# Moving four gate panels from the attention loop into the head norms, the rotation and the turns of a two-block transformer kernel

## The chip, the cores and the metric

The kernel runs on one core of one Trainium2 chip. The metric is the device time of one execution in microseconds; lower is better.

## The reference, cut to what matters

All of it is float32, on 512 rows of width 1024. Two transformer blocks follow each other; the change touches one stretch of the first:

```python
u = rmsnorm(h, mix_norm)
(fq, fk, fv, ff, dq, dk, dv, iq, ik, iw, mq, g) = split(u @ w_in)   # g: 3 x 1024 gate columns
fq, fk = rmsnorm per head                                           # fox attention, 8 heads of 64
dq, dk = rope(rmsnorm per head);  iq, ik = rope(...)                # dsa attention, its index
mq, km = rmsnorm per head                                           # memory attention, 4 heads of 128
score = sum_h iw_h * relu(iq_h @ ik.T)                              # index scores, top 128 per query
o_a, o_b, o_c = fox, dsa (on the chosen keys), memory attention
h = h + sum_n(sigmoid(g_n) * (o_n @ w_branch_n)) @ w_out
```

The change concerns when `g = u @ w_in[:, gates]` is computed. It computes nothing else and leaves nothing out.

## The kernel before, in words

Everything is kept transposed: a tile has 128 features on the partitions and the 512 rows along the free dimension. A weight **panel** is 1024 x 128 (8 blocks of 128 x 128). Its product takes three float32r matmuls per block (`u_hi` with `w_hi`, `u_lo` with `w_hi`, `u_hi` with `w_lo`), 24 of 128x512 in one PSUM bank. A panel passes through a ring of four slots: SP loads `w_raw` (L432), ACT copies it into `w_hi` (`upper_part`, L459), DVE subtracts to make `w_lo` (`lower_parts`, L443), PE multiplies. ACT and DVE prepare panel n + 3 while panel n is multiplied; ACT may write a slot only after the panel that used it is done.

The 3 x 1024 gate columns are 24 panels of this kind. They are not multiplied in a stage of their own: `gate_panels_pe` (L361) is a generator that gives one block (three matmuls, L370 to L372) each time `feed` takes one from it, so that PE has something to do inside stages that wait for other engines. `gate_keep_dve` (L381, the instruction is L389) takes a finished panel out of its bank, `gate_upper` and `gate_lower` prepare the weights of panel m + 3. Gates 0 to 2 stay in SBUF, the others go to DRAM by `store_gate` and come back later. The order of every engine is written out by hand; semaphore counts tie the engines.

The stages around the change, in order of time:

- **mem_q**, the last of the ordinary projections, whose `uppers_act` and `keep_dve` leave gate panels 0 to 2 split.
- **Squares** (`squares_pe`, L750; batch 5, four blocks): ACT squares a head block (L748), PE sums over the features with 4 fp32 matmuls of 2 columns per block (L758) into bank 4. Then ACT takes roots (L764) and DVE one reciprocal (L783).
- **Head norms** (`block_norms_pe`, L766): for 21 blocks PE spreads the inverse roots over a bank (L777, banks 5 and 6 in turn), DVE multiplies (L787).
- **Rotation** (`rotate_pe`, L812): for 10 blocks PE makes the turned copy (L818, banks 4 and 5), DVE does three operations (L824 to L826). PE may start block e when DVE has finished block e - 2.
- **Turns** (`token_pe`, L830; "tokens"): ten groups of transposes (L839 to L845, banks 4 and 5), ACT copies each out (`token_act`, L853 to L863).
- **Index** (`index_pe`, L883): 32 score matmuls (L892), after each one block of a gate panel, after every fourth two: 40 blocks, 5 panels.
- **Attention** (`attend_pe`, L993): 20 steps, one per head: 8 fox, 4 memory, 8 dsa. A step is scores 3 and 2 (L1005), the turns of the step before (L1027), 4 gate blocks, scores 1 and 0, the product of the step before (L1041), 4 gate blocks, one turn. DVE takes maxima, ACT exponentials, POOL multiplies by the inverse sums. 19 gate panels are fed in steps 0 to 18; step 19 has none left.

Panels fed in the index stage and the loop use banks 2 and 3 (`gate_bank`, L323); the attention loop needs banks 0 to 2 for its turns.

Of the kernel before, what the change touches and what calls it, by code (L numbers as in the profile page):

```python
# [34 lines left out]
BANKS = 4  # L35
# [91 lines left out]
def build(nc, T, stop_at=None):  # L127
# [195 lines left out]
    def gate_bank(m):  # L323

        return ps[2 if m in (1, 3) else 3][:, :]
# [35 lines left out]
    def gate_panels_pe(pe):  # L361
        s = segs["gates"]
        for m in range(GATES):
            n = s.base + m
            pe.wait_ge(w_split, n + 1 + RING)
            pe.wait_ge(bank_read, s.group + BANKS + (m - 1 if 1 <= m < 5 else m))
# [14 lines left out]
    def gate_keep_dve(dve, m):  # L381
# [7 lines left out]
        dve.tensor_tensor(out, gate_bank(m), rms[:, :], ALU.mult).then_inc(bank_read, 1)  # L389

# [359 lines left out]
    def squares_pe(pe, blocks, batch, sq, mm):  # L750

        for i, e in enumerate(batch[1], batch[0]):
            x, rows, _, m = blocks[e]
# [12 lines left out]
    def block_norms_pe(pe, blocks, inv, bc, done):  # L766

        pe.wait_ge(inv, 1)
# [43 lines left out]
    def rotate_pe(pe):  # L812
        for e, (x, rows) in enumerate(rotated):
# [4 lines left out]
            pe.matmul(ps[4 + e % 2][0:rows, :], cst[0:rows, C_ROT:C_ROT + rows], x, start=True, stop=True).then_inc(rope_mm, 1)  # L818

    def rotate_dve(dve, st):  # L820
        dve.wait_ge(trig, 3)
        for e, (x, rows) in enumerate(rotated):
# [4 lines left out]
            dve.wait_ge(rope_done, e + 1)  # L827


    def token_pe(pe):  # L830
        pe.wait_ge(rope_done, NR)
        for e in range(10):
            if e >= 2:
                pe.wait_ge(token_done, e - 1)
# [64 lines left out]
    def index_act(act):  # L899
        n = 0  # L900
        for q in range(QB):
            w = (q + 1) * P
            for hh in range(8):
# [4 lines left out]
                if n in INDEX_UPPER:  # L908
                    gate_upper(act, INDEX_UPPER.index(n))
                n += 1  # L910

    def index_dve(dve, st):
        n = 0
        for q in range(QB):
            w = (q + 1) * P
            acc = probs[:, 1, q, :]
            for hh in range(8):
# [8 lines left out]
                if n in INDEX_KEEP:  # L926
                    gate_keep_dve(dve, INDEX_KEEP.index(n))
                if n in INDEX_UPPER:
                    gate_lower(dve, INDEX_UPPER.index(n))
# [63 lines left out]
    def attend_pe(pe, panels):  # L993
# [50 lines left out]
        for n in range(NJ):  # L1044
            scores(n, (3, 2))
            if n:
                turn(n - 1, (1, 0))
            feed(panels, 4)
# [3 lines left out]
            feed(panels, 4)  # L1052
# [4 lines left out]
    def attend_act(act):  # L1057
# [26 lines left out]
        for n in range(NJ):  # L1084
# [3 lines left out]
            if n + 5 < GATES:  # L1088
                gate_upper(act, n + 5)
# [19 lines left out]
    def attend_dve(dve, st):  # L1109
# [6 lines left out]
        for n, j in enumerate(jobs):  # L1116
            for q in DOWN:
                e = QB * n + DOWN.index(q)
                if q == 3:
                    gate_keep_dve(dve, n + 4)  # L1120
# [9 lines left out]
                if q == 2 and n + 5 < GATES:  # L1130
                    gate_lower(dve, n + 5)
# [998 lines left out]
    with block as blk:  # L2130
# [28 lines left out]
        def _(pe):  # L2159
# [14 lines left out]
            squares_pe(pe, head_norms, BATCHES[5], head_sq, head_mm)  # L2174
            block_norms_pe(pe, head_norms, head_inv, head_bc, head_done)
            rotate_pe(pe)
            token_pe(pe)
            panels = gate_panels_pe(pe)
            index_pe(pe, panels)
# [34 lines left out]
        def _(act):  # L2214
# [33 lines left out]
            roots_act(act, head_norms, head_mm, head_rt, root, HEAD_ROOTS)  # L2248
            act.wait_ge(trig, 1)
# [148 lines left out]
```

## Time and profile before

| | us |
|---|---|
| median of 3 runs (2581.49 to 2586.92) | 2586.06 |
| the profiled execution | 2585.37 |
| its span | 2583.6 |
| PE busy in the span | 2462.9 (95%) |
| DVE busy | 1344.5 (52%) |
| ACT busy | 879.4 (34%) |
| mean granted TensorE clock | 0.963 |

The span is what the profiler recorded on the core; 1.8 us lie around it. PE is busy in 95% of it, but a busy PE is not PE at its peak: matmuls are pipelined, and narrow ones (2 columns) count as busy like wide ones. The granted clock is 1.0 at 2.4 GHz and 0.5 at 1.2 GHz.

### The profile page before, as it was taken

To read this page: it belongs to the slowest core of one execution; us is meant where nothing else is said; L and a number is where in the kernel's file an instruction comes from. 1 tells how busy PE (TensorE), PEld (TensorE's weight loads), DVE (VectorE), ACT (ScalarE), POOL (GpSimd) and SP (SyncE) were. 2 spreads that over 40 slices of the span, in tenths; PEclk is the share of its full clock that TensorE was granted. 3 is DMA by queue.
4 is the path that set the end of the run, shared out by engine and by line. 5 is a ranking of instruction groups with operands and counts; after the bars stand their busy time and mean duration, and the time that the engine had idled before them with its cause. 6 is when DMAs were issued, how large, how long until landed. Compare 5 with 4: busy or idle time off the path is not lost.

```text
span 2583.6 us, 32030 instructions
## 1 busy us (share of the span) xinstructions
PE 2462.9 (95%) x12976; PEld 1948.6 (75%) x12976; DVE 1344.5 (52%) x2035; ACT 879.4 (34%) x1453; POOL 120.3 (5%) x156
## 2 busy tenths in 40 slices
PE   7999999997999999999999997888898899999997
PEld 6888888885566668888888886777776687788886
DVE  5444334436557447544433772433374763777723
ACT  4222223321344445322222433334246243433321
POOL 0000000000022210000000000222200000000000
PEclk9999999897999999999999996898898999999998
DMA  5333334330212125333333331000031132233331
GB/s 165 98 98 94 98 97 115 95 82 1 61 58 66 46 98 163 88 94 96 95 104 94 90 83 33 2 2 2 10 91 33 52 96 82 79 95 96 100 97 48
DMA packets 372466, 200.05 MB, mean 77 GB/s; under 512 B 12000, under 2 KB 364512, under 8 KB 372320
## 3 DMA queue, kind: packets, MB, share of 16 engines
q1 hardware_dynamic: 372320, 198.01, 26.5%
q8 instruction: 103, 1.69, 0.3%
q14 instruction: 43, 0.35, 0.0%
HBM read 190.38 MB, written 7.60 MB: 77 GB/s over the span
## 4 chain that ended last, share of the span: by engine, by line
PE 90%; DVE 6%; ACT 3%; issue 1%; DMA 0%; POOL 0%; DVEq 0%; SPq 0%; ACTq 0%
PE ps L510 21%; PE ps L511 21%; PE ps L512 21%; PE ps L370 2%; PE ps L1005 2%; PE ps L758 2%; PE ps L372 2%; PE ps L371 2%; PE ps L1041 2%; PE ps L777 1%; PE ps L2006 1%; PE ps L2008 1%; PE ps L2007 1%; PE ps L892 1%; PE ps L1500 1%; PE ps L1495 1%
## 5 line engine op out<-in xcount | busy, mean ns | idle before, releaser
L510 PE MATMUL ps<-u_hi,w_hi 128*128 128x512 f32 x1608 | 632.1, 393 | 3.0 <-DVE w_lo L443 2.1
L511 PE MATMUL ps<-u_lo,w_hi 128*128 128x512 f32 x1608 | 629.5, 391 | 0.0
L512 PE MATMUL ps<-u_hi,w_lo 128*128 128x512 f32 x1608 | 629.4, 391 | 0.0
L443 DVE TENSOR_TENSOR w_lo<-w_raw,w_hi 128x1024 fp32r<-128x1024 f32 (+2 forms) x366 | 423.0, 1156 | 306.7 <-ACT w_hi L459 305.6
L459 ACT ACTIVATE w_hi<-w_raw 128x1024 fp32r<-128x1024 f32 (+2 forms) x366 | 366.1, 1002 | 461.3 <-PE ps L512 432.6
L510 PEld LDWEIGHTS ps<-u_hi,w_hi 128*128 128x128 f32 x1608 | 300.1, 187 | 72.4 <-DVE w_lo L443 3.0
L511 PEld LDWEIGHTS ps<-u_lo,w_hi 128*128 128x128 f32 x1608 | 300.3, 187 | 67.8 <-issue 2.1
L512 PEld LDWEIGHTS ps<-u_hi,w_lo 128*128 128x128 f32 x1608 | 300.2, 187 | 67.8 <-issue 1.4
L512 PE MATMUL ps<-mid_hi,w_lo 128*128 128x512 f32 x528 | 208.6, 395 | 0.0
L510 PE MATMUL ps<-mid_hi,w_hi 128*128 128x512 f32 x528 | 208.6, 395 | 0.0
L511 PE MATMUL ps<-mid_lo,w_hi 128*128 128x512 f32 x528 | 208.5, 395 | 0.0
L510 PEld LDWEIGHTS ps<-mid_hi,w_hi 128*128 128x128 f32 x528 | 99.1, 188 | 24.1
L511 PEld LDWEIGHTS ps<-mid_lo,w_hi 128*128 128x128 f32 x528 | 99.1, 188 | 24.1
L512 PEld LDWEIGHTS ps<-mid_hi,w_lo 128*128 128x128 f32 x528 | 99.1, 188 | 24.1
L634 ACT ACTIVATE pair_a<-pair_a 128x512 f32<-128x512 f32 x44 | 27.9, 635 | 214.6 <-DVE pair_a L643 214.6
L1105 POOL TENSOR_TENSOR probs<-probs,stat 128x256 f32<-128x256 f32 (+1 forms) x80 | 56.0, 703 | 885.2 <-DVE stat L1114 885.2
L648 DVE TENSOR_TENSOR part<-ps,pair_b 128x512 f32<-128x512 f32 x44 | 30.4, 692 | 126.5 <-PE ps L512 126.4
L370 PE MATMUL ps<-u_hi,w_hi 128*128 128x512 f32 x192 | 84.5, 440 | 0.0
L1286 DVE SCALAR_TENSOR_TENSOR conv_t<-conv_in,vec,conv_t 128x512 f32<-128x512 f32 x108 | 81.0, 750 | 4.6 <-ACT conv_t L1268 2.0
L2092 ACT ACTIVATE conv_t<-conv_in,vec 128x512 f32<-128x512 f32 x44 | 36.0, 817 | 139.0 <-DVE conv_in L2107 139.0
L643 DVE TENSOR_TENSOR pair_a<-ps,rms 128x512 f32<-128x512 f32 x44 | 30.4, 691 | 95.5 <-PE ps L512 95.4
L372 PE MATMUL ps<-u_hi,w_lo 128*128 128x512 f32 x192 | 76.3, 397 | 0.0
(411 smaller groups left out, 3424.3 us busy)
## 6 DMA issues: line engine op xcount, KB each, us to landing
w_raw<-w_in_dram SPq DMA_DIRECT2D x101, 512.0 KB, 3.8
w_raw<-ffn_w_gate_dram SPq DMA_DIRECT2D x44, 512.0 KB, 3.9
w_raw<-ffn_w_up_dram SPq DMA_DIRECT2D x44, 512.0 KB, 3.8
w_raw<-w_up_dram SPq DMA_DIRECT2D x44, 512.0 KB, 3.7
w_raw<-ffn_w_down_dram SPq DMA_DIRECT2D x32, 512.0 KB, 3.7
w_raw<-w_out_dram SPq DMA_DIRECT2D x24, 512.0 KB, 3.6
w_raw<-w_down_dram SPq DMA_DIRECT2D x16, 512.0 KB, 3.6
w_raw<-ffn_w_down_dram SPq DMA_DIRECT2D x16, 384.0 KB, 3.3
```

Of the source, the lines that this page charges most:

```text
L370: pe.matmul(out, wh, u_hi[:, k, :], start=k == 0, stop=False)
L371: pe.matmul(out, wh, u_lo[:, k, :], start=False, stop=False)
L372: mm = pe.matmul(out, wl, u_hi[:, k, :], start=False, stop=k == DK - 1)
L443: dve.tensor_tensor(lo, raw, hi.bitcast(F32), ALU.subtract).then_inc(w_split, 1)
L459: act.activation(w_hi[:, n % RING, 0:blocks, 0:cols], w_raw[:, n % RING, 0:blocks, 0:cols], ACT.Copy).then_inc(hi_done, 1)
L510: pe.matmul(out, wh, h_k, start=k0 + k == 0, stop=False)
L511: pe.matmul(out, wh, l_k, start=False, stop=False)
L512: mm = pe.matmul(out, wl, h_k, start=False, stop=end)
L758: last = pe.matmul(ps[4][:, o:o + 2], square_room[i % 4][0:rows, u * P:(u + 1) * P], m[0:rows, :], start=True, stop=True)
L1005: mm = pe.matmul(bank[:, 0:w], j.q[:, q * P:(q + 1) * P], j.k[:, 0:w], start=True, stop=plain)
L1105: pool.tensor_tensor(x, x, r, ALU.mult).then_inc(sc_norm, 1)
L1286: dve.scalar_tensor_tensor(out=t, in0=x, scalar=v(wcol + n * taps + k), in1=t, op0=ALU.mult, op1=ALU.add).then_inc(conv_done if k == taps ...
```

## The change

Four of the nineteen panels fed in attention are fed earlier. Panels 0 to 3 are multiplied in the squares (one block ahead of each of the 4 squares), ahead of the head norms (6 blocks), in the rotation (2 blocks behind each of the 10 matmuls) and in the turns (2 blocks): 32 blocks. The index stage then multiplies panels 4 to 8, the attention loop panels 9 to 23 in the steps of `FED` (0 to 12, 14 and 16). Steps 13, 15, 17 and 18 now get none, as 19 before. Panels 0 to 8 go round the four banks 0 to 3, which the dense projections used, and wait only for the panel four groups back; from panel 9 on it is bank 3 alone. ACT gets `gate_upper(0)` behind the roots and `gate_upper(1)` to `(3)` behind the sine and cosine; DVE gets `gate_lower(0)` ahead of the reciprocal, and the other new `gate_keep_dve` and `gate_lower` as the diff shows.

```diff
     def gate_bank(m):
-        return ps[2 if m in (1, 3) else 3][:, :]
+        return ps[(segs["gates"].group + m) % BANKS if m <= 8 else 3][:, :]
...
             pe.wait_ge(w_split, n + 1 + RING)
-            pe.wait_ge(bank_read, s.group + BANKS + (m - 1 if 1 <= m < 5 else m))
+            pe.wait_ge(bank_read, s.group + m + (1 if m <= 8 else BANKS))
...
+    FED = tuple(range(12)) + (12, 14, 16)
+    def fed_panel(n):
+        return 9 + FED.index(n)
...
-    def squares_pe(pe, blocks, batch, sq, mm):
+    def squares_pe(pe, blocks, batch, sq, mm, panels=None):
         for i, e in enumerate(batch[1], batch[0]):
+            if panels:
+                feed(panels, 1)
...
-    def block_norms_pe(pe, blocks, inv, bc, done):
+    def block_norms_pe(pe, blocks, inv, bc, done, panels=iter(())):
+        feed(panels, 6)
         pe.wait_ge(inv, 1)
...
             pe.matmul(ps[4 + e % 2][0:rows, :], cst[0:rows, C_ROT:C_ROT + rows], x, start=True, stop=True).then_inc(rope_mm, 1)
+            feed(panels, 2)
...
             dve.wait_ge(rope_done, e + 1)
+            if e == 5:
+                gate_keep_dve(dve, 1)
-    def token_pe(pe):
+    def token_pe(pe, panels):
         pe.wait_ge(rope_done, NR)
         for e in range(10):
+            if e in (3, 6):
+                feed(panels, 1)
...
                 if n in INDEX_UPPER:
-                    gate_upper(act, INDEX_UPPER.index(n))
+                    gate_upper(act, 4 + INDEX_UPPER.index(n))
...
                 if n in INDEX_KEEP:
-                    gate_keep_dve(dve, INDEX_KEEP.index(n))
+                    gate_keep_dve(dve, 4 + INDEX_KEEP.index(n))
                 if n in INDEX_UPPER:
-                    gate_lower(dve, INDEX_UPPER.index(n))
+                    gate_lower(dve, 4 + INDEX_UPPER.index(n))
...
         for n in range(NJ):
+            blocks = 4 if n in FED else 0
             scores(n, (3, 2))
             if n:
                 turn(n - 1, (1, 0))
-            feed(panels, 4)
+            feed(panels, blocks)
             scores(n, (1, 0))
             if n:
                 product(n - 1)
-            feed(panels, 4)
+            feed(panels, blocks)
             turn(n, (2,))
...
-            if n + 5 < GATES:
-                gate_upper(act, n + 5)
+            if n in FED:
+                gate_upper(act, fed_panel(n))
...
-                if q == 3:
-                    gate_keep_dve(dve, n + 4)
+                if q == 3 and (n == 0 or n - 1 in FED):
+                    gate_keep_dve(dve, fed_panel(n - 1) if n else 8)
...
-                if q == 2 and n + 5 < GATES:
-                    gate_lower(dve, n + 5)
+                if q == 2 and n in FED:
+                    gate_lower(dve, fed_panel(n))
...
-            squares_pe(pe, head_norms, BATCHES[5], head_sq, head_mm)
-            block_norms_pe(pe, head_norms, head_inv, head_bc, head_done)
-            rotate_pe(pe)
-            token_pe(pe)
             panels = gate_panels_pe(pe)
+            squares_pe(pe, head_norms, BATCHES[5], head_sq, head_mm, panels)
+            block_norms_pe(pe, head_norms, head_inv, head_bc, head_done, panels)
+            rotate_pe(pe, panels)
+            token_pe(pe, panels)
...
             roots_act(act, head_norms, head_mm, head_rt, root, HEAD_ROOTS)
+            gate_upper(act, 0)
             act.wait_ge(trig, 1)
             act.activation(sinT, ang, ACT.Sin).then_inc(trig, 1)
             act.wait_ge(trig, 2)
             act.activation(cosT, turns_f, ACT.Sin, scale=-1.0).then_inc(trig, 1)
+            for m in (1, 2, 3):
+                gate_upper(act, m)
...
             dve.wait_ge(bank_read, segs["mem_q"].group + 4 + BANKS)
+            gate_lower(dve, 0)
             block_norms_dve(dve, head_norms, head_rt, len(HEAD_ROOTS), root, head_inv, head_bc, head_done)
+            gate_keep_dve(dve, 0)
             rotate_dve(dve, st)
+            gate_keep_dve(dve, 2)
+            for m in (1, 2, 3):
+                gate_lower(dve, m)
             dve.wait_ge(token_done, 12)
+            gate_keep_dve(dve, 3)
```

How the instructions stand, first on PE, from the last rows of the head norms through the start of the rotation. Before, the rotation (L818, `ps<-heads,cst`) is one row of matmuls behind another:

```order
L777 MATMUL ps<-cst,pair_b 64x128 x100
L777 MATMUL ps<-cst,pair_b 128x128 x24
L818 MATMUL ps<-heads,cst 128x512 x4
L818 MATMUL ps<-heads,cst 64x512
L818 MATMUL ps<-heads,cst 128x512 x4
```

In the changed kernel (its L786 and L827 are the L777 and L818 of before):

```order
L786 MATMUL ps<-cst,pair_b 64x128 x100
L786 MATMUL ps<-cst,pair_b 128x128 x24
L827 MATMUL ps<-heads,cst 128x512
L370 MATMUL ps<-u_hi,w_hi 128x512
L371 MATMUL ps<-u_lo,w_hi 128x512
L372 MATMUL ps<-u_hi,w_lo 128x512
L370 MATMUL ps<-u_hi,w_hi 128x512
L371 MATMUL ps<-u_lo,w_hi 128x512
L372 MATMUL ps<-u_hi,w_lo 128x512
L827 MATMUL ps<-heads,cst 128x512
```

Six gate matmuls stand between one rotation matmul and the next.

On DVE, from the last block kept of mem_q (L695) to the head norms, before:

```order
L443 TENSOR_TENSOR w_lo<-w_raw,w_hi 128x1024
L695 TENSOR_TENSOR heads<-ps,rms 128x512
L783 RECIPROCAL pair_b<-pair_b 128x168
L787 SCALAR_TENSOR_TENSOR heads<-heads,vec,ps 128x512 x12
```

and in the changed kernel:

```order
L701 TENSOR_TENSOR heads<-ps,rms 128x512
L449 TENSOR_TENSOR w_lo<-w_raw,w_hi 128x1024
L792 RECIPROCAL pair_b<-pair_b 128x168
L796 SCALAR_TENSOR_TENSOR heads<-heads,vec,ps 128x512 x12
```

A weight split now stands between the last block kept and the reciprocal for which the head norms on PE wait.

On PE in an attention step without panels, in the changed kernel (scores, turns of the step before, scores, first part of the product):

```order
L1019 MATMUL ps<-heads 128x384
L1027 MATMUL ps<-sel,cbf 128x384
L1041 MATMUL ps<-cst,probs 128x128 x7
L1019 MATMUL ps<-heads 128x256
L1027 MATMUL ps<-sel,cbf 128x256
L1019 MATMUL ps<-heads 128x128
L1025 MATMUL ps<-cbf 128x128
L1055 MATMUL ps<-keysT,dvt 64x512
```

This piece stood before in step 19 alone; it now stands in steps 13, 15, 17 and 18 too.

## Rows read from the trace of the kernel before

**Rows 1.** The page: busy time of PE, and its granted clock in 40 slices.

```profile
PE 2462.9 (95%) x12976; PEld 1948.6 (75%) x12976; DVE 1344.5 (52%) x2035; ACT 879.4 (34%) x1453; POOL 120.3 (5%) x156
...
PEclk9999999897999999999999996898898999999998
```

**Rows 2.** Stages: length, busy of PE, PEld, DVE, ACT, POOL, clock, DMA, GB/s.

```profile
574.30:581.30 7.00, 5.53 (x33) 5.43 (x32) 0.69 (x1) 3.47 (x5) 0.00 (x0) 0.72 0.03 8
581.30:583.80 2.50, 0.00 (x0) 0.00 (x0) 1.20 (x1) 2.46 (x8) 0.00 (x0) 0.50 0.00 0
583.80:605.60 21.80, 20.92 (x248) 18.71 (x248) 14.51 (x21) 1.23 (x2) 0.00 (x0) 0.91 0.01 2
605.60:628.70 23.10, 15.26 (x21) 3.56 (x21) 20.69 (x30) 0.00 (x0) 0.00 (x0) 0.78 0.00 1
628.70:636.70 8.00, 6.03 (x32) 4.46 (x32) 0.00 (x0) 5.44 (x12) 0.00 (x0) 0.71 0.00 0
636.70:645.70 9.00, 8.98 (x20) 5.64 (x21) 2.56 (x5) 2.05 (x5) 0.00 (x0) 0.50 0.00 1
645.70:698.10 52.40, 52.40 (x165) 26.14 (x163) 24.09 (x41) 17.48 (x33) 0.00 (x0) 1.00 0.20 55
```

**Rows 3.** Waits of PE, 574 to 960: total us, times, longest.

```profile
PE ps L818 <- DVE heads L826: 4.5, 7, 1.5
PE ps L839 <- DVE heads L826: 3.3, 1, 3.3
PE ps L777 <- DVE pair_b L783: 2.6, 1, 2.6
```

**Rows 4.** Timeline of PE, an earlier batch of four squares: start, us, instruction.

```profile
481.05 1.84 PE L758 MATMUL ps<-cst,pair_a 128*128 128x2 f32 x16
482.75 1.93 PE L758 MATMUL ps<-cst,pair_b 128*128 128x2 f32 x16
```

**Rows 5.** Timeline of ACT and DVE: one weight panel's two halves, and the reciprocal.

```profile
568.97 1.06 ACT L459 ACTIVATE w_hi<-w_raw 128x1024 fp32r<-128x1024 f32 x1 [4.38 <-PE ps L512]
...
570.06 1.23 DVE L443 TENSOR_TENSOR w_lo<-w_raw,w_hi 128x1024 fp32r<-128x1024 f32 x1 [0.46 <-ACT w_hi L459]
...
582.57 1.20 DVE L783 RECIPROCAL pair_b<-pair_b 128x168 f32<-128x168 f32 x1 [7.52 <-ACT pair_b L764]
```

**Rows 6.** Timeline of PE, score matmuls of the index stage.

```profile
636.72 0.79 PE L892 MATMUL ps<-heads 64*128 64x128 f32 x2 [1.46 <-ACT heads L863]
...
646.52 0.49 PE L892 MATMUL ps<-heads 64*128 64x128 f32 x2
...
647.83 0.48 PE L892 MATMUL ps<-heads 64*128 64x128 f32 x2
...
652.44 0.70 PE L892 MATMUL ps<-heads 64*128 64x256 f32 x2
...
687.04 1.12 PE L892 MATMUL ps<-heads 64*128 64x512 f32 x2
...
689.68 1.12 PE L892 MATMUL ps<-heads 64*128 64x512 f32 x2
```

**Rows 7.** Timeline of PE: start of steps 18 and 19.

```profile
922.08 1.12 PE L1005 MATMUL ps<-heads 64*128 64x512 f32 x2
...
935.05 1.12 PE L1005 MATMUL ps<-heads 64*128 64x512 f32 x2
```

**Rows 8.** Step 19: length, busy of PE, PEld, DVE, ACT, POOL, clock, DMA, GB/s.

```profile
935.05:942.60 7.55, 7.42 (x32) 3.74 (x32) 3.05 (x10) 3.96 (x12) 3.19 (x5) 1.00 0.59 188
```

**Rows 9.** PE in single microseconds: length, busy (instructions), granted clock, DMA, GB/s.

```profile
577.00:578.00 1.00, 1.00 (x9) 0.70 0.00 0
...
630.00:631.00 1.00, 1.00 (x6) 0.50 0.00 0
...
632.00:633.00 1.00, 0.78 (x5) 0.99 0.00 0
...
635.00:636.00 1.00, 0.26 (x4) 0.72 0.00 0
```

More of the change, by code:

```diff
@@ L810, in angles_dve, with rotate_pe @@
         dve.sem_inc(trig, 1)
-    def rotate_pe(pe):
+    def rotate_pe(pe, panels):
         for e, (x, rows) in enumerate(rotated):
```

## The prediction

> **What bounds the kernel now.** I read the busy times first: PE 95%, no other engine above 52% [rows 1]. So time is won only where PE waits, or where it runs at the lower clock; the line of granted clocks dips in two neighbourhoods, and the slices 9 to 11 (581 to 646 us and a little around) are the stretch that the change touches. Second, the windows by stage [rows 2]. From the end of mem_q (574) to the first score matmul (636.7) lie 62 us with a granted clock of 0.91 or less; the index stage starts with 9.0 us at 0.50 and is at 1.00 after that. Third, the waits of PE [rows 3]: within the stage it waits for DVE in the rotation (4.5 us), at the end of the rotation (3.3 us) and for the reciprocal (2.6 us). Over all five stages, length less busy time of PE in the windows, it comes to 14.7 us [rows 2]. Last, the attention loop: its dsa steps start at 922.08 and 935.05, 12.97 us apart; step 19, which has no panel, ends its last turn 7.55 us after its start, with PE busy 7.42 of that and the clock at 1.00 [rows 7, 8]. So a fed step is bound by PE's work alone, and the chain of DVE, ACT and POOL in an unfed one fits in PE's own 7.5 us.
>
> **What it removes.** Steps 13, 15, 17 and 18 lose 8 blocks each. The nearest row is step 19: 12.97 - 7.55 = 5.4 us a step, so 4 x 5.4 = 21.6 us. Three corrections. In step 19 the step before was fed, so the probabilities that it turns were long ready; with unfed steps in a row they are fresher. Step 19 already holds the whole chain of its own scores up to its last turn and waits 0.13 us in all, so I take as little again, 0.1 us a step, 0.4 us. In step 15, DVE also splits fox heads (twice two 128x512 operations, each 0.69 us or less by the rotation's 20.69 / 30 [rows 2]). They stand between one maximum and the next, with no gate matmuls left to hide them; 2.8 us is the upper bound and 0 the lower, and I take 1.0, since exponentials and copies of ACT cover part. Nothing saved at all would be the other bound (a step stays at 12.97); I go by step 19, which is the same code. Attention: 21.6 - 1.4 = **20.2 us less**.
>
> **What it adds: 32 blocks**, against the waits above. Stage by stage, at the full clock:
>
> - *Squares.* One square takes (482.75 - 481.05) / 2 = 0.85 us at the full clock [rows 4]. The first block runs in PE's wait for ACT's first square. A gate block among other matmuls costs 0.8 to 0.9 us: in the index stage a step with one block takes 1.31 us (646.52 to 647.83), of which 0.42 are the score [rows 6]. From 575.8: 4 x 0.85 + 3 x 0.8 = 5.8, end at 581.6 against 581.3: +0.3. Before, this stage was at 0.72 of the clock, which is why three more blocks cost so little.
> - *To the reciprocal.* Before, 2.5 us [rows 2]. Now ACT puts a `w_hi` copy (1.06 us) behind the roots, and DVE waits for it and subtracts (1.23 us) ahead of the reciprocal [rows 5]. The head norms wait for that reciprocal, so all of it is on the path: +2.4 with a semaphore. The six blocks (4.2 us) fit into the 4.9. Sum so far +2.7.
> - *Head norms.* PE sets their pace at the full clock (20.92 busy of 21.8 us). Before, the first two or so of 21 ran at 0.5: full clock from the start gives back 1.7. The keep of panel 0 lies beside the first rotation matmul. Sum +1.0.
> - *Rotation.* Before, DVE set the pace: 30 operations, 20.69 us busy in 23.1, so 2.18 us a block [rows 2]. Now PE does one 512-column fp32 matmul and two gate blocks per block. The nearest rows are the last steps of the index stage, 512 columns and two blocks: 687.04 to 689.68, 2.64 us [rows 6]. PE becomes the bound: 9 x 2.64, the last rotation (1.12) and DVE's three operations behind it (2.17), 27.05 us against 23.1. DVE has 0.46 us of slack a block, which takes in the keep (0.69) at block 5. +4.0, sum +5.0.
> - *Turns.* ACT sets the pace with its copies (5.44 of 8.0 us [rows 2]). Two gate blocks (1.7 us) lie beside them; DVE's two keeps and three splits, 2 x 0.69 + 3 x 1.23 = 5.1 us, were idle time of DVE before, and only the last keep comes after the turns, ahead of the first score that DVE waits for anyway. If the blocks were not hidden, +1.7; if the full clock makes the first transposes faster, -1.2. I take 0. Index starts at +5.0.
> - *Index.* The same 40 blocks. Before, the first four steps took 9.8 us (636.72 to 646.52) at 0.50, the next four 5.9 (to 652.44) at 1.00 [rows 6]: 3.9 us are there to be won, if the stage now starts at 2.4 GHz.
>
> DMA: each panel's load waits only for an earlier split, so loads and stores come earlier by up to four panels and nobody waits for them; DMA is at 0.20 in the index stage. The gate rows read back after the loop are stored earlier too. Cost 0.
>
> **The clock decides between three sums.** With 2.4 GHz held in both doubtful places: +5.0 - 3.9 - 20.2 = -19.1 us. If the index stage starts at 1.2 GHz as before: -15.2. If the clock also falls in the squares, where four squares of 2 columns before took it to 0.70 in the microsecond from 577 [rows 9] although PE was "busy": each square and block that remains takes nearly twice as long, about +3.6, for -11.6. For the index: in the turns the clock rose from 0.50 to 0.99 within a run of nothing but transposes (630 to 633), and fell again within the microsecond from 635, though transposes with short waits (0.78 busy in the microsecond from 632) had gone before [rows 9]. Two more gate blocks there do not make it dense, and in the last 1.5 us before the index PE waits for ACT's two copies as before [rows 6]. I take the fall as more likely than not (0.65), the one in the squares as slightly less likely than not (0.45), since 4 of its 7 us are now gate blocks or come right behind them.
>
> The Trainium skill has a rule on this (TensorE: Matmul & The Clock Gate, Part 4: PE-mode transpose): transposes do not count as PE activity for the clock gate and the full clock does not engage in them. By that rule the turns would always lose the clock, and the sum would be -15.2 at best; by the row, where transposes alone raised it, -19.1 stays open. That page and this trace differ, and the trace goes first.
>
> **Forecast.** The profiled execution took 2585.37, 0.7 below the median of 2586.06, so I work from it: 2585.4 - 15.2 = **2570.2 us**.
>
> **The rivals.**
> 1. *Both clocks held:* 2585.4 - 19.1 = 2566.3. For it: every wait in which the clock fell before is now filled or shorter. Against: the turns stay sparse.
> 2. *Both lost:* 2585.4 - 11.6 = 2573.8. For it: squares brought the clock down in this trace each time they ran.
> 3. *Unfed steps are bound by the chain.* In 17, 18 and 19 in a row, the chain maximum, exponential, inverse, POOL, turn, copy is not renewed behind gate matmuls. If a step then takes 10 us instead of 7.55, 4 x 2.4 = 9.8 of the gain go: 2580. Against: in step 19 PE waits 0.13 us in all, ACT is busy 3.96 and POOL 3.19 of 7.55 us [rows 8].
> 4. *Slower: the clock falls in the unfed steps.* What holds it in attention may be the gate matmuls, wide and dense; without them a step has narrow fp32 and transposes. At 0.50 an index step took 9.8 / 5.9 = 1.66 times as long, so a step 7.55 x 1.66 = 12.5, 5.0 more; in all five unfed steps 25 us: 2585.4 - 15.2 + 25 = 2595. It is slower from the fourth such step on. Against: step 19 at 1.00 [rows 8], and the head norms, fp32 with 128 columns alone, came from 0.50 to a mean of 0.91 without any gate block [rows 2].
> 5. *It does not do what it says* is excluded: the order of PE shows 32 blocks in the new places, and four steps without.
>
> **How the numbers follow.** Forecast 0.45 (index alone loses the clock, or the squares alone, nearly the same sum), rival 1 0.17, rival 2 0.26, rival 3 0.08, rival 4 0.04. The range 2562 to 2578: from rival 1 with 4 us more, for turns that run faster and unfed steps without my corrections, to rival 2 with 4 us for a rotation or turns that hide less. It leaves out rivals 3 and 4. A measurement here tells about 0.2%, 5.2 us, from no change. All of the forecast, rivals 1 and 2, and half of rival 3 are faster by more: 0.92; the other half of rival 3: same, 0.04; rival 4: 0.04.
>
> **What would show it.** Right: steps 13, 15, 17, 18 of 7.6 to 8.6 us in the timeline of PE at clock 1.00; rotation matmuls 2.6 us apart, with DVE idle in between; the reciprocal some 2.7 us later; the first score matmul near 641.7, 5 us later than before; the attention loop ending some 15 us earlier. Wrong: unfed steps above 9 us; a half clock in them or in the rotation, where each block would then take over 4 us; a wait of PE on a split weight or a bank in the first gate blocks.

## The result, and the profile after

| | before | changed |
|---|---|---|
| median when the change was first timed | 2583.77 us (4 runs) | 2561.73 us (2556.48 to 2564.09, 4 runs) |
| median in a second series | 2586.71 us (2581.21 to 2588.48, 11 runs) | 2561.85 us (2556.71 to 2566.46, 6 runs) |
| ratio, 95% interval | | 0.9911 [0.9891, 0.9932]; second series 0.9911 [0.9896, 0.9926] |

The change saves 22 to 25 us (0.9%), where 15.2 were forecast; 2561.73 lies 0.3 us below the range. The page of the changed kernel, busy times and granted clock, against [rows 1]:

```profile
PE 2441.7 (96%) x12976; PEld 1937.4 (76%) x12976; DVE 1343.4 (53%) x2035; ACT 878.9 (34%) x1453; POOL 120.5 (5%) x156
...
PEclk9999999999999999999999996988998999999998
```

The dip at slice 10, where the stretch that the change touches begins, is gone in this execution. The digit of slice 8 is 9 instead of 8, but that slice lies ahead of the change and the clock still falls there: it was at 0.5 for some 3 us each from 473 and from 484. The same stages as in [rows 2], now for the changed kernel: squares, wait for the reciprocal, head norms, rotation, turns, index, attention up to step 19. Columns are those of [rows 2].

```profile
573.60:580.90 7.30, 6.53 (x46) 5.68 (x45) 0.69 (x1) 3.48 (x5) 0.00 (x0) 1.00 0.03 8
580.90:585.50 4.60, 4.20 (x18) 3.10 (x17) 2.34 (x2) 4.54 (x10) 0.00 (x0) 1.00 0.00 1
585.50:605.65 20.15, 19.26 (x248) 16.84 (x248) 14.51 (x22) 1.06 (x2) 0.00 (x0) 1.00 0.10 27
605.65:629.90 24.25, 23.37 (x80) 14.44 (x80) 21.97 (x33) 2.12 (x2) 0.00 (x0) 1.00 0.00 0
629.90:637.85 7.95, 5.47 (x38) 4.25 (x38) 4.08 (x4) 5.29 (x12) 0.00 (x0) 1.00 0.63 168
637.85:695.40 57.55, 57.53 (x184) 29.45 (x184) 27.26 (x47) 19.56 (x38) 0.00 (x0) 1.00 0.25 73
695.40:911.60 216.20, 212.31 (x909) 131.90 (x908) 127.11 (x340) 91.14 (x236) 52.80 (x75) 1.00 0.18 55
```

To compare kernels I measure one **stretch** everywhere: from the start of DVE's keep of the last mem_q block (574.35 before, 573.64 after) to the first score of step 19 (935.05, 911.57). It is 360.70 us before and 337.93 in this profile. All numbers of the next table are differences of start times in the profiles; "reciprocal" is from that keep to the first head norm on PE, and the six stages add up to the stretch.

| profile | reciprocal | head norms | rotation | turns | index | attention | stretch |
|---|---|---|---|---|---|---|---|
| before | 9.5 | 21.8 | 23.1 | 8.0 | 61.4 | 236.9 | 360.7 |
| changed (first) | 11.9 | 20.2 | 24.3 | 8.0 | 57.6 | 216.1 | 337.9 |
| changed, again (after_again) | 16.2 | 20.1 | 24.3 | 8.0 | 60.5 | 216.2 | 345.2 |
| changed, third (after_third) | 11.9 | 20.1 | 24.3 | 8.0 | 57.6 | 216.1 | 337.9 |
| changed, fourth (changed_timed) | 11.9 | 20.2 | 24.3 | 8.0 | 62.0 | 216.2 | 342.5 |

The order of the instructions is the same in the last four rows, and four of the six stages repeat to 0.1 us. Only two stages move, and both with the granted clock.

What PE waits for, 574 to 960, changed kernel (total us, times, longest), the largest rows, against [rows 3]:

```profile
PE ps L1041 <- POOL probs L1120: 2.3, 3, 0.8
PE ps L906 <- ACT heads L877: 1.5, 1, 1.5
PE ps L1055 <- ACT keysT L1092: 1.1, 2, 0.8
PE ps L853 <- DVE heads L836: 0.9, 1, 0.9
```

The 4.5, 3.3 and 2.6 us of before have become nothing, 0.9 and 0.4 (the last, the wait for the reciprocal, is a smaller row of the same view).

### The profile page after: what moved, and what is told of

It is laid out like the page before. It is cut to its first block, busy times and chain, and to the rows that moved or that the text cites. A ratio compares the mean times of both kernels' runs of the same rounds, so it can differ in the third digit from the quotient of the medians.

```text
span 2554.7 us, 32031 instructions
## 1 busy us (share of the span) xinstructions
PE 2441.7 (96%) x12976; PEld 1937.4 (76%) x12976; DVE 1343.4 (53%) x2035; ACT 878.9 (34%) x1453; POOL 120.5 (5%) x156
## 4 chain that ended last, share of the span: by engine, by line
PE 91%; DVE 5%; ACT 3%; issue 1%; POOL 0%; DMA 0%; DVEq 0%; SPq 0%; ACTq 0%; POOLq 0%
PE ps L516 21%; PE ps L517 21%; PE ps L518 21%; PE ps L1019 2%; PE ps L370 2%; PE ps L766 2%; PE ps L1055 2%; PE ps L372 2%; PE ps L371 1%; PE ps L786 1%; PE ps L2021 1%; PE ps L2023 1%; PE ps L2022 1%; PE ps L906 1%; PE ps L1515 1%; PE ps L1510 1%
```

## The experiments

### What moving alone does: burst

```diff
-            squares_pe(pe, head_norms, BATCHES[5], head_sq, head_mm, panels)
+            squares_pe(pe, head_norms, BATCHES[5], head_sq, head_mm)
...
-        feed(panels, 6)
+        feed(panels, 32)
...
-            feed(panels, 2)          # rotation
+            feed(panels, 0)
...
-            if e in (3, 6):          # turns
-                feed(panels, 1)
```

> All 32 blocks in one burst between the squares and the head norms, none in the squares, the rotation and the turns; attention as in the changed kernel. Measured from the last block that DVE keeps of mem_q: first score (before 62.4 us, changed 64.2), index stage (61.4, 57.5), attention to the scores of step 19 (236.9, 216.1). Theory (the gain is that PE's waits and low clock are filled): the burst pays for itself, 21.8 us less the 2.5 us wait for the reciprocal and about 1.7 of clock, so first score near 80, the clock falls in the rotation as before and the index stage is 61.4 again, attention 216.1; sum 357 to 358, within 3 us of before. Rival (the attention loop was burdened by more than PE's own time of the panels, so that moving them anywhere wins): sum below 350.

Measured: stretch 360.0 us; first score at +82.2, index 61.7, attention 216.1; 2581.96 us in all beside 2586.91 of before. The stages: squares, burst, norms to turns, index:

```profile
574.40:581.40 7.00, 5.63 (x33) 5.63 (x34) 0.65 (x1) 3.47 (x5) 0.00 (x0) 0.71 0.02 5
581.40:604.60 23.20, 23.20 (x98) 18.83 (x98) 2.34 (x2) 7.83 (x13) 0.00 (x0) 0.94 0.08 23
604.60:656.50 51.90, 40.39 (x301) 24.91 (x300) 40.59 (x58) 5.43 (x12) 0.00 (x0) 0.83 0.11 28
656.50:718.00 61.50, 61.48 (x184) 31.98 (x184) 27.15 (x47) 19.35 (x38) 0.00 (x0) 0.92 0.23 67
```

Attention gives back its 20.8 us and the burst takes all of it; the stretch is 0.7 us shorter than before (2 to 3 us longer than I had computed, since the first score came at +82.2 and not near 80). Moving alone wins nothing in the stretch. What wins is where the same 32 blocks stand in the changed kernel: in waits, and in stages that ran at 1.2 GHz without them. burst does not tell these two apart, as it lost the clock in the squares, in the rotation (at 635.7) and again just ahead of the index stage (at 655.9). The whole run was 5 us below its run of before although the stretch was not; that part is taken up below (Outside the stretch).

### Does it repeat: after_again, after_third

> The changed kernel once more, for how far its stages repeat. If its granted clock is settled by the order of the work, the clock is 1.00 from mem_q to the branches again and the stages repeat within 0.2 us (64.2, 57.5, 216.1). If it was luck of this one execution, the index stage is 61.4 or the squares fall to 0.5 in this one.

> The changed kernel a third time. The first execution held 2.4 GHz from mem_q to the branches (337.9 us from the last kept block to the scores of step 19), the second lost it in the squares and at 643 (345.2). If which of the two comes is settled anew in each execution, this one lies at 337.9, 340.9 (index lost), 342.2 (squares lost) or 345.2, with attention at 216.1 and the rotation at 24.3 in each. If it is the chip that decides, it is 345.2 like the second.

Measured: 345.2, then 337.9 (the table above). In the second profile the clock fell in the squares and once more in the index stage; its stages from the squares to the norms, and the first 9 us of the index:

```profile
576.40:582.40 6.00, 5.99 (x31) 5.57 (x32) 0.00 (x0) 2.81 (x4) 0.00 (x0) 0.68 0.02 3
582.40:591.10 8.70, 8.70 (x29) 7.02 (x29) 2.34 (x2) 5.60 (x11) 0.00 (x0) 0.63 0.13 29
...
643.50:652.50 9.00, 8.98 (x24) 5.45 (x25) 3.17 (x6) 2.06 (x5) 0.00 (x0) 0.62 0.16 52
```

These profiles came from different chips, so by themselves they do not exclude the chip as the cause. Two other things do: of the kernels profiled on the chip of after_again, fed15 and split_behind kept the clock in the squares, after_again and index128 lost it there, and up to that point fed15, index128 and after_again are the same program; and six executions on one chip (changed_timed, below) spread over 9.8 us. So the clock is settled anew in each execution. Losing it in the squares costs 16.16 - 11.86 = 4.3 us, losing it in the index stage 2.9 to 4.4.

### What holds the clock: no_square_blocks, two_in_squares, no_turn_blocks, no_turn_again, one_in_rotation

```diff
# no_square_blocks: squares_pe without panels, and
-        feed(panels, 6)
+        feed(panels, 10)
# two_in_squares
-                feed(panels, 1)
+                feed(panels, 2)
-        feed(panels, 6)
+        feed(panels, 2)
# no_turn_blocks
-            if e in (3, 6):
-                feed(panels, 1)
-        feed(panels, 6)
+        feed(panels, 8)
# one_in_rotation: behind each rotation matmul, and ahead of the norms
-            feed(panels, 2)
+            feed(panels, 1)
-        feed(panels, 6)
+        feed(panels, 16)
```

> The 4 blocks between the squares go behind them (10 ahead of the head norms). Theory (those blocks keep TensorE at 2.4 GHz through the squares): the granted clock falls to 0.5 within the squares as before, squares take 5.5 us instead of the time with blocks, several of the ten blocks run at 1.2 GHz, and the head norms start about 3 us later than in the changed kernel; first score near 67. Rival (the clock does not hang on them): the head norms start within 0.7 us of the changed kernel, first score near 64.2.

> Two gate blocks ahead of each of the four squares, two ahead of the head norms. Theory (the share of wide matmuls between the squares decides whether the clock falls there): the clock stays at 1.00 through the squares; the squares end 2.0 us later (three more blocks on their path), the head norms start at +13.9 instead of +11.9, first score 66.2. Rival (the share does not matter): the clock falls at about 577 and the head norms start after +17.

Measured: without blocks the clock was lost at once and the norms started at +16.9, 5.0 us later than in the changed kernel and not 3; with two, it was held through the squares, the norms started at +13.9 as computed, but then the clock fell in the 2 us in which PE had nothing to do, and the first score came at +67.6 instead of 66.2 (the first line is no_square_blocks' squares; the others are two_in_squares' squares and blocks, its idle time, its first norms):

```profile
574.50:582.00 7.50, 6.09 (x33) 6.09 (x34) 0.69 (x1) 3.66 (x6) 0.00 (x0) 0.68 0.02 6
```

```profile
574.50:586.00 11.50, 10.64 (x62) 8.75 (x60) 0.66 (x2) 5.67 (x13) 0.00 (x0) 1.00 0.02 4
586.00:588.40 2.40, 0.01 (x2) 0.01 (x2) 2.34 (x2) 2.36 (x3) 0.00 (x0) 0.90 0.01 2
588.40:592.00 3.60, 3.60 (x40) 3.60 (x42) 0.92 (x2) 1.05 (x2) 0.00 (x0) 0.59 0.53 144
```

Over all profiles of this study: without a block between the squares the clock was lost in them in 3 of 3 (before, burst, no_square_blocks); with one block each, in 4 of 13; with two, in 0 of 1. That alone is few. The same traces hold more: the four earlier batches of four squares (from 469, 480, 507 and 518 us), which no kernel of this study changes and which have no gate block between them, lost the clock too. It fell some 2 to 5 us after their first matmul in 67 of 68 cases (four batches in 17 profiles). The theory stands, with the addition that one block leaves it to chance; what is said of two blocks rests on one profile.

> The 2 blocks of the turns go ahead of the head norms (8 there). Theory T (the two blocks keep the clock up through the turns): the granted clock falls near the end of the turns and the index stage takes 61.4 us as before. Rival R (the dense rotation does it, the turns are then too short for a fall): the index stage stays at 57.5, first score 63.5 to 65.

> no_turn_blocks a second time. The first lost the clock at 636 and its index stage took 61.9; the changed kernel lost it at 643 in one of three. Theory T (without wide matmuls in the turns the clock falls): index stage 60 or more again. Rival (chance): 57.6.

Measured: index stage 61.9 in both. The first 9 us of it in the first of them:

```profile
636.90:646.00 9.10, 9.10 (x21) 5.67 (x22) 3.24 (x6) 2.06 (x5) 0.00 (x0) 0.50 0.30 90
```

That agrees with T, but it does not tell it apart from chance: with the two blocks in the turns the clock was lost at the start of the index stage in 7 of 9 profiles too (those in which rotation, turns and the way into the index stage stand as in the change; wide_keys, which has one ACT copy fewer there, lost it as well). What the two blocks are worth for the clock stays open. In time they are worth nothing either way: the turns took 6.9 us instead of 8.0, the norms started 0.9 us later, and the first score came at +64.1.

> One block instead of two behind each rotation matmul, the other ten ahead of the head norms (16 there). If PE's time of a 128-row rotation matmul with its blocks is what I now read (0.88 us and 0.68 a block, 2.24 for two), the rotation is bound by DVE again at 2.18 us a block, 0.7 us shorter in all, and the ten blocks ahead of the norms cost 6.8 less the 0.4 us wait: first score near 70. The clock: with PE busy some 1.7 of 2.2 us it holds and the index stage is 57.5; the rival is a fall as before (first score near 71, index 61.4).

Measured: first score +71.9. Norms at +18.2 and the rotation 23.6 us came as computed; PE, timeline, shows DVE in the lead again, 2.17 us apart with a wait before each:

```profile
618.38 1.13 PE L827 MATMUL ps<-heads,cst 128*128 128x512 f32 x2 [0.36 <-DVE heads L836]
620.55 1.07 PE L827 MATMUL ps<-heads,cst 64*64 64x512 f32 x2 [0.35 <-DVE heads L836]
```

The clock fell at 635.6 here, in the last microsecond of the rotation, so that most of the turns ran at 1.2 GHz (10.0 us instead of 8.0), and was back before the index (57.6): neither of my two cases.

### Why the rotation was cheaper than forecast: index128

```diff
-        for b in (B_DKV, B_IKW):
-            act.activation(heads[64:128, b, :], heads[0:64, b, :], ACT.Copy).then_inc(token_done, 1)
+        for x, b in ((heads[64:128, B_DKV, :], B_DKV), (pair_a[64:128, 0, :], B_IKW)):
+            act.activation(x, heads[0:64, b, :], ACT.Copy).then_inc(token_done, 1)
...
-                pe.matmul(..., heads[r, B_IQ + hh // 2, q * P:(q + 1) * P], heads[r, B_IKW, 0:w],
+                pe.matmul(..., heads[:, B_IQ + hh // 2, q * P:(q + 1) * P], idx_keys[hh % 2][:, 0:w],
...
+    idx_keys = (heads[:, B_IKW, :], pair_a[:, 0, :])
...
+            dve.memset(pair_a[0:64, 0, :], 0.0).then_inc(keys_zero, 1)
+            dve.wait_ge(token_mm, 10)
+            dve.memset(heads[64:128, B_IKW, :], 0.0).then_inc(keys_zero, 1)
```

> The index scores use all 128 rows: the stationary block holds two heads, the moving keys are zero in the other head's half (a second key tile, two memsets of DVE). Same products. Theory (a matmul on 64 rows between matmuls on 128 costs about 0.4 us more than one on 128 rows, which is why my price for the rotation was too high): a step of 128 columns takes 0.9 us instead of 1.31, one of 512 columns with two blocks 2.24 instead of 2.64, the index stage 57.5 - 32 x 0.4 = 45 us. Rival (the 0.4 us is the change of kind, fp32 to float32r, and the rotation was cheap for another reason): index stage stays at 57.5.

In the changed kernel's own rotation, eight matmuls are on 128 rows and two on 64 (PE, timeline; `128*128` and `64*64` are rows by columns of the stationary block):

```profile
608.00 1.02 PE L827 MATMUL ps<-heads,cst 128*128 128x512 f32 x2
608.45 0.80 PE L370 MATMUL ps<-u_hi,w_hi 128*128 128x512 f32 x1
...
610.24 1.02 PE L827 MATMUL ps<-heads,cst 128*128 128x512 f32 x2
...
614.82 1.07 PE L827 MATMUL ps<-heads,cst 64*64 64x512 f32 x2
615.82 0.50 PE L370 MATMUL ps<-u_hi,w_hi 128*128 128x512 f32 x1
...
617.31 1.02 PE L827 MATMUL ps<-heads,cst 128*128 128x512 f32 x2
```

A block on 128 rows takes 2.24 us (608.00 to 610.24) and the next gate matmul starts 0.45 us behind it; on 64 rows it takes 2.49 and the gate matmul starts 1.00 behind, and the 64-row matmul itself starts some 0.1 us late (the block before it took 2.33). The index stage has 64-row matmuls only. Two of its steps in the changed kernel, and two in index128:

```profile
645.10 0.49 PE L906 MATMUL ps<-heads 64*128 64x128 f32 x2
...
646.41 0.49 PE L906 MATMUL ps<-heads 64*128 64x128 f32 x2
```

```profile
646.50 0.38 PE L909 MATMUL ps<-heads 128*128 128x128 f32 x2
647.43 0.38 PE L909 MATMUL ps<-pair_a,heads 128*128 128x128 f32 x2
```

1.31 us against 0.93, with the same number of columns and the same kinds of matmul beside it (2.64 against 2.25 for 512 columns and two blocks). Whether the 64 rows were the lower or the upper half made no difference: the steps before take 1.31 in turn. The whole stage took 46.6 us instead of 57.6 to 62.0, 2551.84 us in all. The theory holds; 45 was for the full clock, and this stage began with 3 us at 0.5. wide_and_ahead (below) has the full clock throughout and 43.8 us, but with 38 of the 40 blocks in the stage; with two more at 0.7 us each that is an estimated 45.2.

### Two small terms: fed15, split_behind

```diff
# fed15
-    FED = tuple(range(12)) + (12, 14, 16)
+    FED = tuple(range(13)) + (15, 16)
# split_behind: in block_norms_dve, behind the reciprocal instead of ahead of it
         dve.reciprocal(inverse[:, 0:n], root[:, 0:n]).then_inc(inv, 1)
+        gate_lower(dve, 0)
```

> Steps 15 and 16 are fed, 13, 14, 17, 18 and 19 not. Theory (step 15 took 8.30 instead of 7.61 us because DVE's split of the fox heads stands bare there): all unfed steps take 7.61, fed 15 and 16 12.98, attention 0.7 us shorter (215.4). Rival (the 0.7 us came from the step before or after): no change, the 0.7 us shows in another step.

In the changed kernel, step 15 (875.04 to 883.34, 8.30 us) shows DVE's split ahead of the maxima, and PE's two waits:

```profile
877.64 0.77 DVE L1178 TENSOR_TENSOR o_lo<-heads,o_hi 128x512 fp32r<-128x512 f32 x1
878.33 0.54 DVE L1137 TENSOR_REDUCE stat<-ps 128x1 f32<-128x384 f32 x1
```

```profile
879.64 0.48 PE L1019 MATMUL ps<-heads 64*128 64x128 f32 x2 [0.44 <-ACT probs L1080]
...
880.59 2.34 PE L1055 MATMUL ps<-keysT,dvt 128*64 128x512 f32 x8 [0.31 <-ACT keysT L1092]
```

In fed15 (steps 13 to 17 and the start of 18):

```profile
857.99 1.12 PE L1019 MATMUL ps<-heads 64*128 64x512 f32 x2
865.61 1.12 PE L1019 MATMUL ps<-heads 64*128 64x512 f32 x2
873.22 1.12 PE L1019 MATMUL ps<-heads 64*128 64x512 f32 x2
886.23 1.12 PE L1019 MATMUL ps<-heads 64*128 64x512 f32 x2
899.23 1.12 PE L1019 MATMUL ps<-heads 64*128 64x512 f32 x2
906.84 1.12 PE L1019 MATMUL ps<-heads 64*128 64x512 f32 x2
```

Unfed 7.61, 7.61 and 7.61, fed 13.0: attention 215.5, 0.6 us less. Step 15 costs more only when it is unfed, and DVE's split is what stands bare in it; no run took the split away by itself.

> DVE's split of panel 3 goes behind the reciprocal. Theory (the six blocks hide all but 0.4 us of it): head norms start 0.4 us earlier, first score 63.8. Rival (as I predicted, 1.2 us of it on the path): first score 63.0. Below, no effect.

Measured: norms at +11.4 instead of +11.9, first score +63.8, as the first theory had it. The run (2561.62 us) lost the clock in the index stage, so its total says nothing of 0.4 us.

### Can the start of the index be filled: ahead_of_index

```diff
     def index_pe(pe, panels):
+        feed(panels, 2)
         pe.wait_ge(token_done, 12)
...
-                feed(panels, 2 if n % 4 == 3 else 1)
+                feed(panels, (2 if n % 4 == 3 else 1) if n < 31 else 0)
```

> Two of the 40 blocks of the index stage go ahead of its wait for ACT's two copies, after the last turns. Theory (PE idles 1.5 us there, and that idle time is what brings the clock down at the start of the index stage): first score at most 0.1 us later than 64.2, the index stage 1.5 us shorter (56.0) and at 1.00 throughout. Rival (the fall comes from the turns themselves): 1.5 us shorter at full clock, but the clock falls again between 636 and 645 and the stage takes 59 to 60.

Measured: the first score came at +68.6, because this execution lost the clock in the squares. The index stage stayed at 1.00 and took 56.8 us, but attention took 219.4, 3.2 more. I had taken the two blocks from behind the last score. There PE now waits bare for ACT, 0.69 us, and the clock falls in the first attention step (index, boundary, step 0):

```profile
644.00:700.00 56.00, 56.00 (x179) 28.38 (x178) 26.45 (x46) 18.15 (x36) 0.00 (x0) 1.00 0.25 74
700.00:703.00 3.00, 2.31 (x7) 0.91 (x6) 2.11 (x5) 1.88 (x2) 0.00 (x0) 0.86 0.00 0
703.00:709.00 6.00, 6.00 (x16) 3.98 (x14) 4.13 (x11) 2.40 (x5) 1.04 (x1) 0.50 0.12 44
```

A miss with a lesson: the blocks behind the last score were a cover. The theory itself gained by it: both profiles with two blocks ahead of the index's wait (this one and wide_and_ahead) kept the clock there, against 2 of 9 without them.

### The version that the runs point to: wide_keys, wide_and_ahead

```diff
# wide_keys: index128, and for the dsa heads (a zeroed copy of the keys in the place of the index keys)
-        j.kind, j.rows, j.q, j.k = "dsa", r, heads[r, B_DQ + b, :], heads[r, B_DKV, :]
+        j.kind, j.rows, j.q, j.k = "dsa", r, heads[r, B_DQ + b, :], heads[:, B_IKW if hh % 2 else B_DKV, :]
+        j.wide = heads[:, B_DQ + b, :]
# wide_and_ahead: wide_keys, fed15, split_behind, and
+        feed(panels, 2)          # ahead of index_pe's wait
-                feed(panels, 2 if n % 4 == 3 else 1)
+                feed(panels, 2 if n % 4 == 3 and n > 7 else 1)
```

> As index128, and the dsa scores of attention use 128 rows too, with a second key tile that is zero in the other half. In the index stage alone 128 rows took 0.92 instead of 1.31 us a step. Theory (each switch between 64 and 128 rows costs): a dsa step has two pairs of fp32 score matmuls beside 128-row matmuls in each half, so 4 x 0.2 to 4 x 0.4: fed steps 11.4 to 12.2 instead of 12.98, unfed ones at least as much shorter than 7.61 as the chain allows (6.5 to 7.3); attention 216.1 - 8 x 1.2 = 206 to 210. Rival (a bf16 matmul on 128 rows behind it hides the switch, or the chain of DVE, ACT and POOL bounds the step): less than 0.3 us a step, attention above 213.

Measured: fed dsa steps 11.9 to 12.0, unfed ones 7.02; attention 211.1, outside my 206 to 210. About 1.0 us a fed step is there, but only 0.6 an unfed one: those now wait for ACT's copies (PE, waits 840 to 915):

```profile
PE ps L1059 <- ACT keysT L1098: 2.9, 6, 0.8
```

So both were half right: the switch of rows costs in attention too, and below 7.0 us the chain bounds an unfed step.

> wide_keys with three more edits: steps 15 and 16 fed and 14 not (0.7 us), DVE's split of panel 3 behind the reciprocal (0.4), two of the index stage's blocks ahead of its wait, taken from behind its fourth and eighth score and not from the last (1.4). wide_keys took 326.4 us for the stretch with both clocks lost, so about 319 with both held; less 2.5. Theory: stretch 317 to 324, median 2541 to 2546, 40 to 45 below before. Rival (dsa steps are now bound by ACT's copies, so the edits in attention give nothing, and the denser index stage loses the clock more): 325 or more, less than 37 below before.

Measured: **2541.57 us** median (2541.28 to 2542.34, 4 runs), ratio to before 0.9831 [0.9818, 0.9844]; it beats both kernels. Its stretch is 317.8, with the clock at 1.00 in every stage. Its four runs lie within 1.1 us, where those of the changed kernel spread over 9.8: with the blocks ahead of the index's wait and those behind its last score left in place, the outcome at these two places seems to be settled; the squares still have one block each, so part of it can be luck. The stages (to the norms, norms to turns, index, attention):

```profile
574.70:586.10 11.40, 10.63 (x64) 8.78 (x62) 2.96 (x3) 7.56 (x15) 0.00 (x0) 1.00 0.01 2
586.10:638.40 52.30, 49.48 (x373) 36.62 (x373) 42.20 (x61) 8.41 (x15) 0.00 (x0) 1.00 0.14 37
638.40:682.20 43.80, 43.80 (x179) 32.14 (x178) 26.92 (x47) 19.00 (x38) 0.00 (x0) 1.00 0.32 95
682.20:892.40 210.20, 205.23 (x903) 132.82 (x908) 126.72 (x340) 91.81 (x238) 52.79 (x75) 1.00 0.18 57
```

### The second series: changed_timed

> The changed kernel against the one before, five rounds, and its profile a fourth time. In the three profiles so far the stretch took 337.9 twice and 345.2 once (before: 360.7). Theory (the clock in the squares and in the index stage is settled anew in each execution, everything else repeats): its own runs spread over some 8 us, the median is 20 to 26 us below before, and this profile shows 337.9, 340.9, 342.2 or 345.2. Rival (my forecast of 15 us was right and the first runs were lucky): the median is 14 to 18 us below.

Measured: 24.9 us below before (2586.71 - 2561.85); its own runs spread over 9.8 us; stretch 342.5, the start of the index stage alone at the lower clock. That is the case that I had put at 340.9: the loss in the index stage cost 4.4 us here and not the 2.9 of after_again. The theory stands, the rival falls. Before's median was 2583.77 in the first series and is 2586.71 here: its runs lie near 2581.5 or near 2587, 2 and 2 in the first series, 3 and 8 in this one.

## Why the prediction was wrong, step by step

The measured median lies 8.5 us below the forecast of 2570.2. The four profiled executions of the changed kernel have a mean of 2560.2, 25.2 us less than the profile of before from which I worked: 19.8 of it in the stretch, where I had 15.2, and 5.3 behind it, where I had nothing. Two terms failed: the rotation was sized wrong, and the rest of the program was put at 0 without a row.

- **Attention: 20.2 less. Right.** 20.8 measured. Steps 13, 17 and 18 took 7.61, 7.61 and 7.61, step 15 8.30; I had 7.65 and 8.65. That the extra belongs to an unfed step 15 is shown by fed15.
- **Squares and reciprocal: +2.7. Right** at the full clock: +2.4, with PE left waiting 0.4 us for the reciprocal where I had 0.7. With the clock lost: +6.7, where I had +6.3.
- **Head norms: -1.7. Right:** -1.7.
- **Rotation: +4.0. This step failed; it was +1.2.** I took the price of a rotation matmul from the nearest index row, 2.64 us for 512 columns and two blocks [rows 6], and overlooked that this row's matmul is on 64 rows (`64*128`) while eight of ten rotation matmuls are on 128. On 128 rows it is 2.24: the nine starts that I had at 9 x 2.64 = 23.8 us took 20.7 (605.65 to 626.36). index128 shows that the number of rows makes the difference. The mechanism was right, as PE sets the pace, but it is hardly slower than DVE's 2.18.
- **Turns: 0. Right:** 7.95 against 8.0, as a balance of two terms that I had named and not added up: no_turn_blocks shows 6.9 us at the full clock without blocks, so the full clock gave back 1.1 and the two blocks cost 1.0.
- **Index: -3.9, if the clock holds. Right** when it held (57.6).
- **The clock.** The three sums were the right shape, and both places are chance: lost in the index in 7 of 9 profiles with the turns as in the change (I had 0.65), in the squares in 4 of 13 (0.45). But every sum was 3.0 to 3.9 too high: -22.8 measured for -19.1 where both held, -18.2 (fourth profile) for -15.2 and -15.5 for -11.6 where the index or both were lost. 2.8 of that is the rotation, 0.6 attention, the rest the reciprocal and what the lost clock cost (4.4 in the index stage of the fourth profile, 2.9 in the second, where I had 3.9).
- **Outside the stretch.** The four stretches of the changed kernel save 22.8, 15.5, 22.8 and 18.2, mean 19.8; the medians differ by 22.0 and 24.9. The rest lies behind attention, where no instruction was changed: about half of it (2.5 of 5.4 us in the first profile) has been gained when the last solve matmul of the second block's delta rule starts (L1490, 899.3 us behind step 19 before; L1505, 896.7), the rest behind that. The first line of each is the 620 us behind the stretch, the second the next 440; before, then changed:

```profile
935.05:1555.05 620.00, 619.09 (x2698) 502.56 (x2698) 343.83 (x450) 206.79 (x282) 3.19 (x5) 1.00 0.36 104
1555.05:1995.05 440.00, 380.35 (x3759) 323.20 (x3757) 196.02 (x356) 184.71 (x393) 64.09 (x72) 0.87 0.09 24
```

```profile
911.57:1531.57 620.00, 619.09 (x2699) 502.83 (x2699) 343.33 (x449) 207.12 (x283) 3.19 (x5) 1.00 0.35 101
1531.57:1971.57 440.00, 379.94 (x3781) 322.95 (x3779) 195.70 (x356) 185.85 (x397) 64.33 (x72) 0.89 0.09 24
```

  From the first score of step 19 to the end it was 1648.6 us before and 1643.1, 1644.2, 1643.0 and 1642.8 in the four profiles of the changed kernel. There is one profile of before, and the other kernels of this study had 1642.4 to 1647.0, burst 1645.8 with a stretch that saved nothing. So this is no gain that the change owns for sure: the runs of before themselves lie in two groups, 3 of 11 near 2581.5 and 8 near 2587, and the one profile, of a run of 2585.37, stands near the upper one. Why the clock falls as it does there stays open. My range took every spread from inside the stretch and none from outside; with the rotation's 2.8 us that is why 2561.7 fell out of it.
- **The rivals.** The chain-bound rival fell (7.61 us in a row), and so did the slower one: the clock was 1.00 in all unfed steps. The Trainium skill (TensorE: Matmul & The Clock Gate, Part 4: PE-mode transpose) says that the full clock does not engage for transposes; by that rule the turns would always lose the clock. The traces do not bear this out as it stands: two of the four profiles of the changed kernel held 1.00 through the turns and on, and in no_turn_blocks, whose turns are nothing but transposes (629.98 to 635.45), the clock was at 1.00 until it fell at 636.7, in the wait ahead of the index stage. Whether transposes help to hold it stays open, as it was lost at that place with the two blocks and without.

## What to carry to other kernels

Work moved into waits wins as much as the waits hold, and the same work in one burst won nothing here; the price of an instruction must come from a row with the same number of rows and columns, not only of columns. Where a stage mixes narrow and wide matmuls near the point at which the clock falls, give a forecast per clock outcome, profile the same kernel more than once, and look at the whole trace for how much the rest of it moves by itself. Keys that two heads share can be multiplied on all 128 rows with zeros in the other head's half, which took an estimated 12 us off the index stage and 5 off attention, both bound by PE.

## What the runs showed of the hardware that I had not expected

- An fp32 matmul on 64 rows between float32r matmuls on 128 costs 0.38 us more than one on 128 rows with the same columns (1.31 against 0.93 us for 128 columns with one block), though it does half the work.
- The same program got 1.2 GHz or 2.4 GHz in the same place from one execution to the next: 345.2 and 337.9 us for one stretch, repeating to 0.1 us where the outcome was the same.
- 0.69 us of bare wait at the border of two dense stages went with a fall to 1.2 GHz that cost 3.2 us; in the other 16 profiles, where two blocks follow the last score, it did not fall there. Two blocks in the 1.5 us wait ahead of the index stage went with a held clock in 2 of 2 profiles, against 2 of 9 without.
- Four squares (fp32 matmuls of 2 columns) in a row keep PE busy without a gap between 480 and 485 us, and yet such batches went with a fall to 1.2 GHz in 67 of 68 cases ahead of the stretch, and in 3 of 3 inside it.
